# Moving one ACT cast, one gate activation and the order of the output norm's root inside a gated-delta-rule head

## The reference

```python
def gdn_scan(q, k, v, g, beta, s0):
    ...
    sol = lax.linalg.triangular_solve(a_strict, rhs, left_side=True, lower=True, unit_diagonal=True)
    u, w = sol[..., :V], sol[..., V:]
    attn = jnp.einsum('bhcik,bhcjk->bhcij', q, k) * decay
    ...
    def step(S, inp):
        qd, ke, ui, wi, ai, dec = inp
        v_new = ui - jnp.einsum('bhqk,bhkv->bhqv', wi, S)
        o = jnp.einsum('bhqk,bhkv->bhqv', qd, S) + jnp.einsum('bhqs,bhsv->bhqv', ai, v_new)
        S = S * dec[..., None, None] + jnp.einsum('bhsk,bhsv->bhkv', ke, v_new)
        return S, o

def gdn_out_norm(o, z, w):
    bsz, L = o.shape[:2]
    o = o * lax.rsqrt(jnp.mean(o * o, axis=-1, keepdims=True) + EPS) * w.astype(jnp.float32)
    return o.reshape(bsz, L, GDN_WIDTH) * jax.nn.silu(z.astype(jnp.float32))
```

## Time and profile before

| | |
|---|---|
| runs | 3173.44, 3143.82, 3142.83 us |
| median | 3143.82 us |
| profiled execution | 3173.44 us, span 3171.6 us |
| PE busy | 3096.1 us (98%) |
| DVE busy | 1919.3 us (61%) |
| ACT busy | 1380.4 us (44%) |
| mean granted TensorE clock | 0.993 of full speed |

### The profile page before, as it was taken

How to read it: one execution, slowest core, us unless ns; L and a number is a source line. 1 busy time by engine, 2 the same in 40 slices (tenths; PEclk the granted TensorE clock), 3 DMA queues, 4 the chain that set the end, 5 groups by cost and what they waited for, 6 DMA issues and landing times.

```text
span 3171.6 us, 68708 instructions
## 1 busy us (share of the span) xinstructions
PE 3096.1 (98%) x28830; PEld 2899.8 (91%) x28830; DVE 1919.3 (61%) x2548; ACT 1380.4 (44%) x1758; POOL 184.2 (6%) x281
## 2 busy tenths in 40 slices
PE   6999999999999999999999999999999999999999
PEld 1587788788898999999999999999999999999999
DVE  6666667667787666555555554566665554555544
ACT  5545454444445445443333333444444333333332
POOL 0000000000010000211000000200002110000000
PEclk9999999999999999999999999999999999999999
DMA  9612112122394444455555555555445555555554
GB/s 353 257 68 81 69 68 82 70 79 92 138 371 176 177 172 173 176 194 190 198 188 197 190 194 194 190 205 179 174 159 183 186 187 185 186 186 185 186 185 146
DMA packets 79939, 544.59 MB, mean 172 GB/s; under 512 B 8325, under 2 KB 12437, under 8 KB 15264
## 3 DMA queue, kind: packets, MB, share of 16 engines
q1 hardware_dynamic: 76272, 519.08, 45.2%
q10 hardware_dynamic: 2768, 19.66, 1.6%
q0 software_dynamic: 736, 3.46, 0.3%
HBM read 537.94 MB, written 4.22 MB: 171 GB/s over the span
## 4 chain that ended last, share of the span: by engine, by line
PE 87%; DVE 6%; issue 4%; ACT 2%; DMA 0%; POOLq 0%; DVEq 0%; ACTq 0%; POOL 0%
PE bank L418 27%; PE bank L419 26%; PE bank L420 26%; DVE w_lo L402 2%; PE bank L736 1%; ACT w_hi L397 1%; PE bank L633 1%; PE bank L668 1%; PE bank L677 1%; PE bank L627 1%; DVE s_acc L1475 0%; PE bank L833 0%; PE bank L1010 0%; DVE g_L L1626 0%; PE bank L816 0%
## 5 line engine op out<-in xcount | busy, mean ns | idle before, releaser
L397 ACT CAST w_hi<-raw 128x2048 fp32r<-128x2048 f32 x477 | 910.5, 1909 | 1307.1 <-PE bank L420 1271.4
L402 DVE TENSOR_TENSOR w_lo<-raw,w_hi 128x2048 fp32r<-128x2048 f32 x477 | 1096.8, 2300 | 576.3 <-ACT w_hi L397 576.0
L418 PE MATMUL bank<-a_lo,w_hi 128*128 128x256 f32 (+1 forms) x3664 | 1099.4, 300 | 9.2 <-DVE w_lo L402 7.9
L419 PE MATMUL bank<-a_hi,w_lo 128*128 128x256 f32 (+1 forms) x3664 | 1074.1, 293 | 0.0
L420 PE MATMUL bank<-a_hi,w_hi 128*128 128x256 f32 (+1 forms) x3664 | 1073.7, 293 | 0.0
L418 PE MATMUL bank<-h_lo,w_hi 128*128 128x256 f32 x3584 | 1005.5, 281 | 0.7
L419 PE MATMUL bank<-h_hi,w_lo 128*128 128x256 f32 x3584 | 995.2, 278 | 0.0
L420 PE MATMUL bank<-h_hi,w_hi 128*128 128x256 f32 x3584 | 995.0, 278 | 0.0
L418 PEld LDWEIGHTS bank<-a_lo,w_hi 128*128 128x128 f32 x3664 | 695.3, 190 | 34.3 <-DVE w_lo L402 10.1
L420 PEld LDWEIGHTS bank<-a_hi,w_hi 128*128 128x128 f32 x3664 | 691.9, 189 | 19.8
L419 PEld LDWEIGHTS bank<-a_hi,w_lo 128*128 128x128 f32 x3664 | 692.1, 189 | 15.4 <-issue 0.5
(11 more groups left out here) (327 smaller groups left out, 2012.7 us busy)
## 6 DMA issues: line engine op xcount, KB each, us to landing
raw<-stream SPq DMA_DIRECT2D x485, 1024.0 KB, 4.8
gate_raw<-stream ACTq DMA_DIRECT2D x16, 1024.0 KB, 7.0
xr<-x_t SPq DMA_DIRECT2D x4, 1024.0 KB, 16.4
turned<-by_distance POOLq DMA_DIRECT2D x1, 2048.0 KB, 12.5
x_res<-x_t SPq DMA_DIRECT2D x1, 2048.0 KB, 17.5
bias_table<-bias SPq DMA_DIRECT2D x1, 2048.0 KB, 10.9
bias<-bias_table ACTq DMA_DIRECT2D x1, 2048.0 KB, 9.5
out_t<-x_res SPq DMA_DIRECT2D x4, 512.0 KB, 5.1
```

Of the source, the lines that this page charges most:

```text
L397: act.copy(w_hi[u.slot][:], raw[u.raw][:]).then_inc(hi_ready, 1)
L402: dve.tensor_tensor(w_lo[u.slot][:], raw[u.raw][:], w_hi[u.slot][:], ALU.subtract).then_inc(lo_ready, 1)
L418: pe.matmul(acc, wh, lo[:, k, 0:n], start=(k == first), stop=False)
L419: pe.matmul(acc, wl, hi[:, k, 0:n], start=False, stop=False)
```

## The change

Three instructions move on ACT, and one piece of filler moves on PE, in each of the 8 heads:

- the cast of unit u+8 goes from behind the copies of step 2 to behind the level 6 copies, ahead of the copies of step 0
- silu of the gate takes its place behind the copies of step 2 (it stood behind the square of the output)
- silu of the next head's k is no longer linked. The table load comes before the wait for `oss`, and Ln and Exp of the output norm come before the squares of k and q
- the two blocks of filler ahead of PE's wait for `osq_ready` go behind the `oss` matmul

```diff
@@ -844,10 +844,9 @@
                 m.then_inc(S["o_mm"], 1)
-                ahead(3, 13, 15)
                 pe.wait_ge(S["osq_ready"], i + 1)
                 mm(psum[5][:, 0:L], ONES, g_X[:, 0:L], start=True, stop=True).then_inc(S["oss"], 1)
-                ahead(3, 15, KT)
+                ahead(3, 13, KT)
@@ -1134,6 +1133,7 @@
                             act.copy(half, d3(psum[6 + d][r, L:2 * L], 64)).then_inc(S["ut_ready"], 1)
+                        split_act(act, u.ahead(8))
                     if level == 2:
@@ -1153,17 +1153,16 @@
                     if step == 2:
-                        split_act(act, u.ahead(8))
+                        f(gate, gate, ACT.Silu)
                 act.wait_ge(S["o_mm"], i + 1)
                 f(g_X[:, 0:L], psum[4][:, 0:L], ACT.Square).then_inc(S["osq_ready"], 1)
-                f(gate, gate, ACT.Silu)
                 if more:
-                    own.link(silu(i, 1, 1))
+                    silu(i, 1, 1)
+                act.preload_act_table_set(LOG_EXP)
                 act.wait_ge(S["oss"], i + 1)
+                root(g_M[0][:, L:2 * L], psum[5][:, 0:L], g_M[0][:, 0:L], 1.0 / P, "o_rs")
                 if more:
                     squared()
-                act.preload_act_table_set(LOG_EXP)
-                root(g_M[0][:, L:2 * L], psum[5][:, 0:L], g_M[0][:, 0:L], 1.0 / P, "o_rs")
```

## The result

The changed kernel takes 3166.66 us (median of 20 runs, 3159.76 to 3197.99) against 3142.64 us before (20 runs, 3139.0 to 3173.44). The ratio is 1.0078, 95% interval 1.0056 to 1.0099: 24 us slower, where the forecast was 14.7 us. The time lies inside the forecast's range of 3148 to 3167 us, by 0.3 us.

What follows compares the result with a forecast made beforehand. PE's in-order instruction stream was taken to bound the kernel. Step 0 (8 x 1.13 = 9.0 us), boundaries (7 x 0.71 = 5.0 us) and the last head (0.7 us) gave 14.7 us: 3143.8 + 14.7 = 3158.5 us, range 3148 to 3167.

Steps and rivals of the forecast that it cites:

- all three new waits: PE waits in each head: about 1.3 us at line 841, 0.7 us at line 849, 0.4 us at line 721.
- the chain at the boundary is the bound: Rival: the ACT-DVE chain between heads holds PE, so earlier Exp gains 8.9 us; about 3145 us, chance 0.12.
- bound for what a shorter chain can give: Between heads: at most PE's wait for u+5's low part, 0.40 us at seven boundaries, 2.8 us.
- Part 1: The cast ahead of step 0 delays ACT's copies, so line 816 starts 1.13 us later per head.
- DVE's cover: At step 0: DVE's state copies start late because the level 6 convolution holds DVE, which absorbs part of the delay.
- The boundary: Between heads: the first block of u+5 starts 0.71 us later, at seven boundaries, 5.0 us.
- the wait at u+5: PE's old wait at line 418 for u+5's low part vanishes, giving back 0.40 us per boundary.
- Idle 0.40: PE's idle time per head, in us, waiting for the low part of u+5 in the kernel before.
- Part 2: Filler moved behind oss: PE idles about 0.70 us for the square of the output, and what follows starts later.
- the falls: Rival: new PE pauses in each head make the granted clock fall, 1.7 us each; 3172 us, chance 0.12.
- the rival's 13.6 us: Extra time if the clock fell in each head: 8 x 1.7 us; chance 0.12.
- The drain: Rival: about 1.38 us on top of each table switch at the head's end; 3168 us, chance 0.01.

Runs made afterwards that it cites:

- e3: The kernel before with only the head's end on ACT reordered as after, the cast still in step 2: 3148.58 us against 3145.23 us.
- e7: The kernel before with only the gate's silu moved behind the cast of step 2: 3143.95 us against 3144.41 us.
- e8: The kernel before with gate silu in step 2, silu of k behind step 3's copies, squares in own columns ahead of the table load: 3140.43 us against 3143.32 us.
- e1: The kernel before with only the cast of u+8 moved ahead of the copies of step 0: 3169.34 us against 3145.23 us.
- e2: The kernel before with only the two blocks of filler moved behind the oss matmul: 3145.54 us against 3145.23 us.
- e11: The kernel after with one filler block moved from behind oss into step 0, ahead of the wait for ACT's copies: 3156.35 us against 3144.41 us before.
- e10: The kernel before with all filler behind oss and the cast behind the copies of step 3: 3150.98 us against 3144.41 us.
- e6: The kernel after with two filler blocks moved from behind oss into step 0, ahead of the wait for ACT's copies: 3158.44 us against 3143.32 us before.
- e9: e8 with the last filler block moved into step 0 behind the products with v_new: 3135.74 us against 3143.32 us, again 3134.64 us against 3144.41 us.

## Why the prediction was right, and where its sizes were off

**The direction and the stalls.** PE is the stream that counts, and all three new waits stand where the text put them. The head was forecast at 1.84 us more and takes 1.87 us more. The rival "the chain at the boundary is the bound" falls: Exp ends 1.3 us earlier against `o_mm` and nothing is gained (e3 is slower, e7 is no change). Its argument against is the one that held, u+5's cast waits for `g_ss`. The text's bound for what a shorter chain can give was too low, though: e8 gets 0.64 us per boundary and not 0.40.

**Two terms were off and offset each other.** Part 1 was forecast at 1.13 us and is 1.53 - 0.03 = 1.50 us (e1: 1.47 us per head). The cast began 0.1 us later than reckoned (0.79 us behind the start of the `g_U` copies and not 0.67), its start-to-start time there is 1.92 and not 1.81 us, and DVE's cover of about 0.25 us doesn't exist: from line 841 to 816 it is 1.00 us before and 0.97 us after. I had worked out when the first product would be in PSUM from half of line 841's time and took the rest for slack. The boundary was forecast at 0.71 us and is 0.4 us, because the wait at u+5 gives back 0.64 us (1.89 to 1.25 us from start to start) and not 0.40 us. "Idle 0.40" is counted from the modelled end of the matmul before it, and a matmul's end lies behind the point where the next one could start. By the same token line 841's 1.38 us of idle time are 1.53 us lost. Part 2 alone thus costs 0.06 us per head (e2), where the text's method gave 0.3. That 1.84 and 1.87 us agree so well is therefore luck in part.

**What the sum left out is the clock.** The text gave the falls a chance of 0.12 and 1.7 us each, as a rival. They came in 6 of 8 heads at 1.27 us each, 7.6 us in the trace and some 9 to 12 us by the runs. Without them the forecast would have been near; with them the time is at the very end of its range. The argument against them was that PE is busy for 3.79 of 5 us at 675 us, that the clock stays, and that "the forecast's heads have no denser ones". This last step doesn't hold by the rows of before:

```profile
343.00:348.00 5.00, 4.64 (x44) 4.10 (x41) 3.58 (x8) 3.57 (x9) 0.00 (x0) 1.00 0.44 184
```

PE is busy for 4.64 us around step 0. Less the 1.3 us that line 841 was to wait, 3.3 us are left, which is under the 3.79 us, and after shows 3.37. As for the pause itself, the trace of before had a fall behind 2.03 us and none behind pauses of 1.2 and 1.4 us near 677 and 686 us. By their length the forecast's 1.3 us looked safe, but the length alone is no guide. With rows for and against it a chance near one half would have been fitting, and half of the rival's 13.6 us would have made the forecast some 21 us. The Trainium skill, TensorE: Matmul & The Clock Gate, "Why this matters for your kernels", warns of idle gaps of PE between bursts of matmuls, but of longer ones. Here after and e1 show falls behind gaps of 1.4 us, and the measurement decides. The price of a fall was taken too high, 1.7 us (half of 3.4 us) for the measured 1.27. One part of the difference shows in the trace: in a head without a fall PE waits for DVE in this stretch (line 816 of step 2, 0.22 us of idle time), and in five of the six heads with one this is 0 to 0.12 us. Where the rest comes from isn't shown.

**The table load.** Ln starts 0.01 us after the load's end at 366.83 also where the load stands ahead of the wait. The load itself starts 0.01 us after the end of the silu before it (365.54). The drain that the Trainium skill, ScalarE: Activation LUTs, counts in "What ACT_TABLE_LOAD costs" is not seen at this load.

**What stays open.** Why the same pause brings a fall in six heads and none in the other two. What besides the pause's length decides: e11 shows that at step 0 a pause shorter by 0.35 us is enough to lose the falls, and line 907 that a pause of the same length elsewhere brings none, but no run varies what stands around a pause while keeping its length. Between after and e11 the runs differ by 12 us and the traces by 8 us. The intervals of the two runs are wide enough for that.

## What to carry to other kernels

An instruction that can run "any time" costs most of its length (here 1.5 of 1.9 us) where it stands ahead of a short link of a PE-ACT-DVE-PE chain, however idle its engine is over the whole span: look for the slot whose idle time, before the next wanted instruction, is longer than it (here 2.9 us in step 2). Filler placed in a wait for another engine doesn't bring the awaited result earlier (833 to 841 takes 2.61, 2.61 and 2.62 us with one, two and three blocks in it). It pays only if it comes from a place where it stood on the path, or if it keeps the clock up. Price a pause of PE by the distance of starts, and then ask what the clock did behind the nearest pauses of that size in the trace.

## What was not expected of the hardware

- A pause of 1.38 us of PE among spaced small matmuls is followed by 3.4 us at 1.2 GHz in 6 of 8 cases (4 of 8 in e1). Pauses of 1.04, 0.70 and 0.50 us at the same place are not, nor are 1.28 us at the head's end (e10) and 1.41 us at line 907.
- Pauses of 1.9 to 2.1 us at line 736 come 17 times in the 14 traces. At 15 of them the clock falls, in e6 (1.98 us) and once in e10 (1.92 us) it doesn't.
- In the profiled execution of before PE fed 4% fewer matmuls than after in the same 500 us, at a granted clock of 1.00 and with no wait. The same 4% show in single units: the 48 matmuls of u+4 take 5.84 us in e9 and 5.64 us in e8. What slows PE is not in the profile.
